# Two entries of an issue order: the next tile's key normalisation one stage later, output products ahead of the transposes

## The reference, cut to what matters

```
kk = kk / max(sqrt(sum(kk * kk)), 1e-12)           # per head: "the key normalisation"
def step(s, inp):
    r_t, w_t, k_t, v_t, kk_t, a_t = inp
    sa = einsum('bhij,bhj->bhi', s, -kk_t)
    s = s * w_t[:, :, None, :] + sa[..., None] * (kk_t * a_t)[:, :, None, :] \
        + v_t[..., None] * k_t[:, :, None, :]
    return s, einsum('bhij,bhj->bhi', s, r_t)
o = (o - mu) * lax.rsqrt(var + GN_EPS) * gain + bias + sum(r * k * rk) * v
```

## Time and profile before

| | |
|---|---|
| median of 3 runs | 2236.63 us |
| span of the profiled execution | 2378.0 us |
| PE busy | 2170.7 us, 91% of the span |
| DVE busy | 1077.5 us, 45% |
| ACT busy | 682.4 us, 29% |
| POOL busy | 226.2 us, 10% |
| mean granted TensorE clock | 0.937 of full speed |

### The profile page before, as it was taken

How to read it: one execution, slowest core, us unless ns; L and a number is a source line. 1 busy time by engine, 2 the same in 40 slices (tenths; PEclk the granted TensorE clock), 3 DMA queues, 4 the chain that set the end, 5 groups by cost and what they waited for, 6 DMA issues and landing times. The chain is left out here.

```text
span 2378.0 us, 55745 instructions
## 1 busy us (share of the span) xinstructions
PE 2170.7 (91%) x24578; PEld 1400.4 (59%) x24578; DVE 1077.5 (45%) x2577; ACT 682.4 (29%) x1853; POOL 226.2 (10%) x225
## 2 busy tenths in 40 slices
PE   8999899997899988999989998899888999899998
PEld 4655577774565655664456555777645656556543
DVE  2034157764565444443320331677636644444433
ACT  1231144442454411110012311444425543111100
POOL 0000000010000132202100000010000001222022
PEclk9999988987999988899999999999979998888999
DMA  5110000000003154442111101000000032544321
GB/s 186 45 59 22 36 3 4 4 4 20 1 1 80 45 220 170 171 152 71 59 55 45 58 22 36 3 4 4 4 20 1 1 81 75 196 171 167 108 71 64
DMA packets 49843, 150.85 MB, mean 63 GB/s; under 512 B 15106, under 2 KB 19458, under 8 KB 40132
## 3 DMA queue, kind: packets, MB, share of 16 engines
q1 hardware_dynamic: 37316, 71.79, 9.2%
q0 software_dynamic: 12288, 75.51, 8.7%
HBM read 129.70 MB, written 12.86 MB: 60 GB/s over the span
## 5 line engine op out<-in xcount | busy, mean ns | idle before, releaser
L373 PE MATMUL psum<-work 128*128 128x368 f32 (+1 forms) x1632 | 514.1, 477 | 9.2 <-DMA work<-w_z 6.8
L373 PEld LDWEIGHTS psum<-work 128*128 128x128 f32 (+1 forms) x1632 | 307.4, 189 | 212.3 <-issue 25.7
L2191 PE MATMUL psum<-work,mixed 128*128 128x512 f32 (+1 forms) x576 | 248.8, 592 | 1.6 <-PEq L1863 1.6
L2191 PEld LDWEIGHTS psum<-work,mixed 128*128 128x128 f32 (+1 forms) x576 | 106.2, 186 | 137.7 <-issue 137.7
L1932 PE MATMUL psum<-work,ub 32*64 32x256 f32 x2048 | 145.9, 443 | 39.9 <-issue 35.7
L2059 DVE STREAM_TRANSPOSE work<-work 128x1024 f32<-128x1024 f32 x128 | 150.5, 1214 | 0.4 <-issue 0.3
L1635 ACT ACTIVATE work<-psum,work 128x128 f32<-128x128 f32 (+8 forms) x130 | 97.8, 752 | 157.0 <-DVE work L1738 155.4
L1519 PE MATMUL psum<-work 96*128 96x512 f32 (+3 forms) x384 | 139.2, 496 | 3.7 <-ACT work L1635 2.1
L1803 POOL DMA_INDIRECT work<-cache_ckv,pages x64 | 60.6, 948 | 757.8 <-PE psum L1469 386.0
L2069 DVE TENSOR_REDUCE work<-psum 128x1 f32<-128x1024 f32 x32 | 39.2, 1225 | 205.5 <-PE psum L1932 205.5
L1932 PEld LDWEIGHTS psum<-work,ub 32*64 32x64 f32 x2048 | 71.5, 148 | 97.9 <-issue 91.6
(11 more groups left out here) (260 smaller groups left out, 3270.2 us busy)
## 6 DMA issues: line engine op xcount, KB each, us to landing
work<-w_z SPq DMA_DIRECT2D x4, 2560.0 KB, 11.3
work<-w_out SPq DMA_DIRECT2D x4, 2048.0 KB, 9.3
xres<-work SPq DMA_DIRECT2D x16, 512.0 KB, 2.9
work<-xT SPq DMA_DIRECT2D x4, 1104.0 KB, 8.9
work<-x_tok SPq DMA_DIRECT2D x8, 512.0 KB, 4.1
work<-xres SPq DMA_DIRECT2D x8, 512.0 KB, 4.3
work<-w_z SPq DMA_DIRECT2D x1, 2304.0 KB, 12.4
o_ckv<-ckv SPq DMA_DIRECT2D x2, 1104.0 KB, 4.3
```

Source lines behind the costliest of these rows:

```text
L373: return nc.tensor.matmul(zb[i % 2][n][rows, 0:G], z_weights(m, g)[:, k, lo:lo + Z_W[i]], xT[:, k, span(n)], start=k == 0, stop=k == DK - 1)
L2191: last = nc.tensor.matmul(yb[t % 2][half][0:n, :], m.mixed[:, k, lo:lo + n], wo[half][:, k, :], start=k == 0, stop=k == DK - 1)
```

## The change

Two entries of the table `BESIDE` move. `unit` of tile t+1 goes from the end of stage `mid` to stage `zf`, behind the last chunk's `read`. In stage `wu`, `out` goes ahead of `flip`. No instruction is added or removed and no operand changes.

```
-    "mid": [("write", -1, 2), ("gate", -2, 0), ("unit", 1, 0)],
-    "zf": [("read", -1, 3), ("keys_decay", 1, 0)],
-    "wu": [("write", -1, 3), ("flip", 1, 0), ("out", -1, 0)],
+    "mid": [("write", -1, 2), ("gate", -2, 0)],
+    "zf": [("read", -1, 3), ("unit", 1, 0), ("keys_decay", 1, 0)],
+    "wu": [("write", -1, 3), ("out", -1, 0), ("flip", 1, 0)],
```

## The result

The changed kernel took 2219.02 us (median of 4 runs, 2217.5 to 2221.23), against 2236.4 us before: a ratio of 0.9913, 95% interval 0.9892 to 0.9935. A second set gave 0.9915 (0.9884 to 0.9945; 6 runs, 2218.54 to 2233.86, against 25 of before), where 0.989 to 0.992 and no fall of the clock in the ordinary steps were expected.

What follows compares the result with a forecast made beforehand. DVE bounds full-clock steps between `wu` and `proj`, PE the low-clock and tenth steps. Terms -7.4 (clock), -0.5 (first steps), -1.4 (tenth steps), +0.4 (small costs) make -8.9 us, scaled -8.4: 2228.2 us, range 2220 to 2239.

Steps and rivals of the forecast that it cites:

- The move of `unit` and of `out`: Ordinary steps: PE idle before `wu` falls from 0.85 to 0.06 us; new stall of 0.43 before `prod`; 1.00 before `proj`.
- The 0.03 us of `unit`: DVE's path: sum L1231 waits 0.03 us for the last `read`, in 14 steps: +0.4 us.
- Nothing at full clock: Full-clock steps gain nothing: `prod` ends 0.36 us earlier, but `proj` waits for DVE; PE's idle time stays 1.49 us.
- Through the clock: Ordinary steps: four of five clock falls at `wu` go, at 1.85 us each: -7.4 us.
- My best case of 9.25 us: Ordinary steps: at best all five clock falls at `wu` go, 5 x 1.85 = 9.25 us saved.
- The ends of the block: First steps of the layers save 0.25 us each (0.5 us), tenth steps 0.7 us each (1.4 us).
- The scale: Whole sum: -8.9 us on the profiled span times 0.9405, the runs' median over that span, gives -8.4 us.
- The 141 us: Whole kernel: the 2378.0 us profiled span exceeded the runs' median by 141 us; no row said where, so it scaled.
- The waits only move: Rival: falls continue as often, or unprofiled runs hold none; only -1.5 us remain, scaled -1.4: 2235.2 us; chance 0.33.
- PE is the bound: Rival: L1182 waits for `prod` in ordinary steps too; 5.8 us more saved, scaled -13.8: 2222.8 us; chance 0.16.
- The new gaps drop the clock: Rival: stalls before `prod` and `proj` lower the clock; seven falls give +12.0, scaled +11.3: 2247.9 us; chance 0.09.

Runs made afterwards that it cites:

- `fill`: Kernel before, its order kept, with three unread 128 x 128 identity products on PE ahead of the wait before `wu`: 2216.97 us, 0.9894 of before.
- `gap_back`: Changed kernel plus one wait: PE starts `wu` only after the first instruction of `unit`, idle 1.10 us before it: 2247.21 us, 1.0021 of before.
- `unit_only`: Kernel before with only `unit` moved to stage `zf`; `flip` stays ahead of `out`: 2225.69 us, 0.9937 of before.
- `out_only`: Kernel before with only `out` moved ahead of `flip`; `unit` stays where it was: 2243.53 us, 1.0016 of before.
- `fill_one`: Kernel before with one unread 128 x 128 product on PE ahead of the wait before `wu`, 0.43 us left idle: 2225.85 us, 0.9937 of before.
- `mix_z2`: Changed kernel with `mix` (2.0 us of DVE) moved from stage `wt` to behind `finish` in stage `z2`: 2246.38 us, 1.0015 of before.

## Why the prediction was right in its mechanism and wrong in its size

**The move of `unit` and of `out`.** Right, to a few hundredths: 0.06 us forecast before `wu`, about 0.05 measured; 0.43 before `prod`, 0.51 measured; 1.00 before `proj`, 0.98 measured; L1182 unmoved. The 0.03 us of `unit` on DVE's path show too: 7.27 us against 7.24.

**Nothing at full clock.** Right. `fill` and `gap_back` show it from both sides: a gain comes without either move, and goes with both in place. The full-clock steps two to eight average 22.48 us before (second profile) and 22.40 in the changed kernel.

**Through the clock.** This is the term that failed, in size: -7.4 us for the sixteen ordinary steps. Summed, they took 366.5 us in the first profile of before and 368.9 in the second, 353.4 and 355.3 in the two of the changed kernel, so 11 to 16 us less. I took four falls of five; all went, and there were six in the second profile. And I took 1.85 us each from one slow step and one quick one. In the second profile the six slow steps average 24.80 us, and the fourteen ordinary steps of 336.51 to 493.27 and 1445.57 to 1602.43 in the changed kernel average 22.40: a fall costs 2.40 us. Six of them are 14.4 us. My best case of 9.25 us was no bound for the same two reasons. I had also misread one row: the ninth step at 499.96, 22.53 us long, is not of the ordinary make-up but has fewer products, and the ninth step that held its clock lasts 20.11 us (1686.37 to 1706.48), so that this fall cost 2.4 us and did not leave the step at the length of a full-clock one.

**The ends of the block.** Mis-sized too, and again by the clock. For the tenth steps I had 0.7 us each by the path. Where the low stretch covers the same last 5.4 us of the step, it lasts 17.40 us before (first profile, second layer) and 16.72 after (second profile, first layer), so 0.7 us is right as far as this pair goes. But I had noted the 1.45 us idle before that `wu` and not asked for its falls. In the second profile of before, the tenth steps:

```profile
523.76:543.05 19.29, 16.07 (x541) 13.41 (x541) 10.23 (x35) 6.21 (x18) 1.01 (x1) 0.71 0.01 3
1641.88:1662.81 20.93, 18.35 (x540) 15.17 (x541) 10.14 (x35) 6.21 (x18) 1.01 (x1) 0.58 0.01 3
```

They sum to 40.2 us, in the two profiles of the changed kernel to 34.8 and 34.6. Now 0.42 us are idle there instead of 1.45:

```profile
1622.34 1.08 PE L897 MATMUL psum<-work 32*32 32x128 f32 x32 [0.42 <-DVE work L1201]
```

That is up to 5.6 us for a term of 1.4; the falls of the clock there, some 4 us, I had put at nothing. The first steps sum to 43.8 and 43.1 us before, 43.4 and 43.1 after, which neither bears out my 0.5 us nor denies it.

So the step of the prediction that failed is the price of the clock: 7.4 us, and nothing in the tenth steps, where the profiles show about 14.4 us in the ordinary steps and some 4 us in the tenth. These sizes come from single profiles, which differ by 20.5 us inside the steps; the medians of the two sets of runs differ by 17 and 15 us.

**The scale.** Multiplying by 0.9405 took half a microsecond off for no reason. The 141 us were outside the block, in the two stretches of score products. Both layers had them (208.81 and 211.06 us), so comparing the layers would not have told me that they were unusual; only a second profile does.

**The rivals.** "The waits only move" was right on the waits and wrong on what they do. Its rule from the Trainium skill ("TensorE: Matmul & The Clock Gate", "A second HAM failure mode: psum-queue depth-cycling") would have short pauses drop the clock by their frequency; here the change made more pauses of about the same sum, and the falls went from six to none. So the place matters: 0.95 us behind `write` (`unit_only`) and 0.98 us before `proj` were followed by no fall, 0.85 us among the small products of the inverse by some. What about the place does it, the size of the products or the other waits near by, is not shown. "PE is the bound" fell, since a span and a device time are 2 us apart and L1182 waits for nobody in a full-clock step. "The new gaps drop the clock" fell, with no fall at either.

How much of the whole is the clock can also be read from the runs. Over 71 runs of the kernel before, which had clocks of 0.946 to 0.961, the time goes down by 1468 us for a clock higher by 1 (a straight line; correlation -0.90). From a mean of 0.9540 to the 0.9634 of ten runs of the changed kernel that makes 13.8 us, of the 17.8 between the means of their times. This is a correlation and carries no cause by itself; the cause rests on `fill` and `gap_back`.

## What to carry to other kernels

Where TensorE does long chains of small products, look for a wait of most of a microsecond, or several shorter ones close together, in their midst and for a step with a granted clock under 1, even if the engine has slack there: the wait can cost more in the steps after it than it lasts. Test it cheaply by filling it with products that nobody reads. If that makes the kernel faster and the low stretches go, reorder so that the wait falls behind larger products, and do not move other work of the waited-for engine into the chain.

A count of idle time with no releaser shown belongs beside the count of falls, since steps of the same make-up at full clock differed by up to 0.9 us by it.

Predict the clock's part from more than one profile, since the number of falls differs from run to run, and compare a profile's span with the time of its own execution before scaling anything.

## What the runs showed of the hardware that I had not expected

- A wait of about 0.85 us among small products was followed by 6.8 us at half clock in five and in six of sixteen steps of the same make-up (the two profiles of before), and in one of fifteen in `out_only`; 1.10 us in eight of sixteen (`gap_back`). At 0.43 us (`fill_one`) it did not happen there. It did at 0.42 us in the changed kernel's first step, with waits of 0.84 and 0.40 us just ahead.
- 1.13 us among the small products, in `mix_z2`, dropped the clock thirteen times in sixteen steps.
- Unread products on PE made a kernel 1.06% faster (`fill`, interval 0.82 to 1.29%).
- Steps of the same instructions, all at full clock, lasted 21.99 us without and 22.66 to 22.86 us with an idle time of PE that has no releaser in the profile (second profile of before). Its cause is open.
- The same program once took 143 us longer, all in the two stretches of the score products (419.9 us against 276.4), with DVE and ACT as busy as in the second profile, PE busy 378.3 us against 274.6, and a granted clock of 0.87 and 0.86 against 0.98. Its cause was not looked into.
